# Second expert matrices on a DMA queue of their own, issued by GpSimd, in a two-block float32 kernel

## The reference, cut to what matters

```python
D_MODEL, N_EXPERTS, TOP_K, D_FF_2 = 1024, 32, 4, 1024
w1 = nrm((L, N_EXPERTS, D_MODEL, 2 * D_FF_2), D_MODEL ** -0.5)
w2 = nrm((L, N_EXPERTS, D_FF_2, D_MODEL), DEEPNORM_BETA * D_FF_2 ** -0.5)
...
f = moe_ffn(h.reshape(-1, D_MODEL), w_router[l], b_router[l], w1[l], b1[l], w2[l], b2[l]).reshape(x.shape)
x = layer_norm(DEEPNORM_ALPHA * x + gt2 * f, ln2_g[l], ln2_b[l])
```

## Time and profile before

| | |
|---|---|
| Time, median of 3 runs | 2309.51 us (2307.12 to 2314.98) |
| The profiled execution: its time, its span | 2312.77 us, 2311.0 us |
| TensorE busy over the span | 2213.1 us, 96% |
| VectorE, ScalarE, GpSimd busy | 706.0, 357.4, 100.3 us |
| Granted TensorE clock, mean | 0.979 |
| DMA, whole execution | 582.13 MB, mean 252 GB/s |
| DMA in the last 17 of 40 slices | 411 to 426 GB/s in all but the first and the last |

### The profile page before, as it was taken

The page is one execution under the profiler, slowest core; times in us unless marked ns, Lnnn a source line. Parts: engine busy times, 40 slices in busy tenths (PEclk is TensorE's granted clock), DMA queues, the critical chain, the costliest instruction groups (busy, mean ns, idle before and its releaser), DMA issues.

```text
span 2311.0 us, 34017 instructions
## 1 busy us (share of the span) xinstructions
PE 2213.1 (96%) x15007; PEld 1368.3 (59%) x15008; DVE 706.0 (31%) x1186; ACT 357.4 (15%) x771; POOL 100.3 (4%) x114
## 2 busy tenths in 40 slices
PE   7999999999999998989998998999999999999997
PEld 6767686888577775567887653344344444434432
DVE  0000101621275415347777532112111121121113
ACT  1000200240100012243434111001000010100000
POOL 1000000000100000112221000000000000000000
PEclk9999899999999999999999989999999999999999
DMA  9655444244678951000001379999999999999996
GB/s 319 192 158 184 145 138 145 82 137 161 221 237 273 285 189 55 1 3 3 3 22 48 149 313 419 426 426 424 417 424 426 425 426 411 417 425 426 425 425 271
DMA packets 199428, 582.13 MB, mean 252 GB/s; under 512 B 9620, under 2 KB 153808, under 8 KB 166384
## 3 DMA queue, kind: packets, MB, share of 16 engines
q1 hardware_dynamic: 194656, 564.70, 63.5%
q0 software_dynamic: 4208, 13.27, 1.5%
q10 hardware_dynamic: 416, 1.96, 0.2%
HBM read 576.49 MB, written 3.42 MB: 251 GB/s over the span
## 4 chain that ended last, share of the span: by engine, by line
PE 90%; DVE 5%; DMA 2%; ACT 1%; issue 1%; SPq 0%; ACTq 0%; DVEq 0%
PE ps L2561 22%; PE ps L605 13%; PE ps L2573 10%; PE ps L664 8%; PE ps L614 7%; PE ps L1333 5%; PE ps L2540 3%; PE ps L2588 2%; PE ps L795 2%; PE ps L768 2%; PE ps L1660 2%; PE ps L1680 1%; PE ps L1762 1%; PE ps L969 1%; DMA arena<-in_w 1%; PE ps L1677 1%
## 5 line engine op out<-in xcount | busy, mean ns | idle before, releaser
L2561 PE MATMUL ps<-ring,const 128*64 128x512 f32 (+1 forms) x1536 | 472.0, 594 | 0.8 <-ACT const L2315 0.8
L2561 PEld LDWEIGHTS ps<-ring,const 128*64 128x64 f32 (+1 forms) x1536 | 160.6, 144 | 307.4 <-issue 306.1
L605 PE MATMUL ps<-arena,ring 128*128 128x256 f32 x1408 | 313.4, 381 | 2.6 <-issue 2.6
L605 PEld LDWEIGHTS ps<-arena,ring 128*128 128x128 f32 x1408 | 264.7, 190 | 47.3 <-issue 12.9
L2561 PE MATMUL ps<-arena,const 128*64 128x512 f32 (+1 forms) x512 | 225.2, 593 | 0.0
L2573 PE MATMUL ps<-ring,const 128*64 128x512 f32 (+1 forms) x768 | 190.3, 594 | 0.8 <-DMA ring<-in_w 0.8
L664 PE MATMUL ps<-arena,ring 128*128 128x256 f32 x800 | 174.5, 381 | 1.3 <-issue 1.3
L664 PEld LDWEIGHTS ps<-arena,ring 128*128 128x128 f32 x800 | 153.0, 191 | 22.5 <-issue 1.5
L2775 DVE TENSOR_SCALAR arena<-ps 128x1024 f32<-128x1024 f32 x18 | 22.0, 1225 | 458.5 <-PE ps L2561 458.4
L614 PE MATMUL ps<-ring,arena 128*128 128x512 f32 x352 | 157.6, 592 | 0.0
L2573 PEld LDWEIGHTS ps<-ring,const 128*64 128x64 f32 (+1 forms) x768 | 65.2, 143 | 112.6 <-issue 111.1
(11 more groups left out here) (485 smaller groups left out, 2458.8 us busy)
## 6 DMA issues: line engine op xcount, KB each, us to landing
ring<-in_w SPq DMA_DIRECT2D x96, 2048.0 KB, 17.7
ring<-in_w SPq DMA_DIRECT2D x96, 1024.0 KB, 15.2
arena<-in_w SPq DMA_DIRECT2D x32, 2048.0 KB, 19.9
ring<-in_w_in SPq DMA_DIRECT2D x26, 1536.0 KB, 6.9
arena<-in_w SPq DMA_DIRECT2D x32, 1024.0 KB, 17.5
ring<-in_w_ada SPq DMA_DIRECT2D x16, 1536.0 KB, 9.0
ring<-in_ffn_w_gate SPq DMA_DIRECT2D x44, 512.0 KB, 4.0
ring<-in_ffn_w_up SPq DMA_DIRECT2D x44, 512.0 KB, 5.4
```

The lines of the kernel that those rows point to most:

```text
L605: ins = pe.matmul(ps[:, j % 2, half * S:(half + 1) * S], s[:, col0:col0 + P], uT[:, k, :], start=(k == 0), stop=(k == KD - 1))
L2561: ins = pe.matmul(ps[a * n:(a + 1) * n, q, :], xsT[:, k, a * n:(a + 1) * n], chunk(chunks[a])[:, q * 512:(q + 1) * 512], start=False, stop ...
```

## The change

The second matrices leave SyncE's list. A new function `moe_pool`, called last in GpSimd's program, goes through the blocks and issues their loads on GpSimd's own DMA queue (q0 in the profile; SyncE's is q1). Slots, chunk numbers, sizes and `room` stay as they are. The landings of second matrices are counted on eight semaphores of their own, one for each of the four chunk positions and for even and odd blocks; TensorE waits once for the chunks of both experts in place of once for each.

```diff
@@ chunk_tables
-        pieces += [W2_AT[s - 1] + i for i in range(KD // 2 * len(BLOCKS[s - 1]))] if s else []
@@ build
-        def w2_load(e, n, expert, c):
+        def w2_load(e, n, expert, c, landed_sem):
             e.dma_start(chunk(n).rearrange("p (j n) -> p j n", j=2),
-                        x["w2_2"][0, expert, 2 * c * P:2 * (c + 1) * P, :].rearrange("a (p j) n -> p (a j) n", j=2)).then_inc(*landing(n))
+                        x["w2_2"][0, expert, 2 * c * P:2 * (c + 1) * P, :].rearrange("a (p j) n -> p (a j) n", j=2)).then_inc(landed_sem, 16)
+
+        def second_landing(s, c):
+            return sems(f"w2_landed{s % 2}_{c}"), 16 * sum(len(BLOCKS[b]) for b in range(s % 2, s + 1, 2))
...
+        def moe_pool(e):
+            for s in range(NBLK):
+                blk = BLOCKS[s]
+                if s == 1:
+                    e.wait_ge(*at("cnt", 1))
+                expert = {}
+                for r in blk:
+                    expert[r] = bass.ds(e.value_load(ids[0:1, r:r + 1], min_val=0, max_val=NE - 1), 1) if s else slice(r, r + 1)
+                for c in range(KD // 2):
+                    for a, r in enumerate(blk):
+                        n = W2_AT[s] + c * len(blk) + a
+                        room(e, n)
+                        w2_load(e, n, expert[r], c, second_landing(s, c)[0])
@@ moe_sync
-                if s:
-                    blk = BLOCKS[s - 1]
-                    for c in range(KD // 2):
-                        for a, r in enumerate(blk):
-                            n = W2_AT[s - 1] + c * len(blk) + a
-                            room(n)
-                            w2_load(e, n, expert[r], c)
@@ moe_pe, second
-                    for a in range(w):
-                        moe_landed(pe, W2_AT[s] + c * w + a)
+                    pe.wait_ge(*second_landing(s, c))
@@ gpsimd
             load_last(p)
+            moe_pool(p)
```

More of the change, by code:

```diff
@@ L2479, in w1_load @@
                         x["w1_2"][0, expert, 2 * c * P:2 * (c + 1) * P, :].rearrange("a (p j) n -> p (a j) n", j=2)).then_inc(*landing(n))
-        def w2_load(e, n, expert, c):
+        def w2_load(e, n, expert, c, landed_sem):
             e.dma_start(chunk(n).rearrange("p (j n) -> p j n", j=2),
-                        x["w2_2"][0, expert, 2 * c * P:2 * (c + 1) * P, :].rearrange("a (p j) n -> p (a j) n", j=2)).then_inc(*landing(n))
-        def moe_sync(e, turns):
[L2486 to L2504, removed]
-                    if s:
-                        for r in blk:
-                            expert[r] = bass.ds(e.value_load(ids[0:1, r:r + 1], min_val=0, max_val=NE - 1), 1)
-                    for c in range(KD // 2):
-                        for a, r in enumerate(blk):
[L2510 to L2513, removed]
-                    blk = BLOCKS[s - 1]
-                    for c in range(KD // 2):
-                        for a, r in enumerate(blk):
-                            n = W2_AT[s - 1] + c * len(blk) + a
-                            room(n)
-                            w2_load(e, n, expert[r], c)
@@ new lines, in w2_load, with room @@
+                        x["w2_2"][0, expert, 2 * c * P:2 * (c + 1) * P, :].rearrange("a (p j) n -> p (a j) n", j=2)).then_inc(landed_sem, 16)
+        def second_landing(s, c):
+            return sems(f"w2_landed{s % 2}_{c}"), 16 * sum(len(BLOCKS[b]) for b in range(s % 2, s + 1, 2))
+        def room(e, n):
+            if n < 2:
+                pass
+            elif n < 8:
+                e.wait_ge(*at("v_end", 4))
+            elif n < 14:
+                e.wait_ge(*at("out2_0", 2))
+            elif n < MC:
+                e.wait_ge(*at("xhat", 2))
+            else:
+                e.wait_ge(*at("m_used", USED_AT[n - MC]))
@@ new lines, in moe_sync @@
+        def moe_sync(e, turns):
+            for s in range(NBLK):
+                blk = BLOCKS[s]
+                if s == 1:
+                    e.wait_ge(*at("cnt", 1))
+                expert = {}
+                for r in blk:
+                    expert[r] = bass.ds(e.value_load(ids[0:1, r:r + 1], min_val=0, max_val=NE - 1), 1) if s else slice(r, r + 1)
+                for c in range(KD // 2):
+                    for a, r in enumerate(blk):
+                        n = W1_AT[s] + 2 * (c * len(blk) + a)
+                        room(e, n + 1)
+                        w1_load(e, n, expert[r], c)
@@ L2526, in more @@
                 for c in range(KD // 2):
-                    w2_load(e, KD + c, one, c)
+                    w2_load(e, KD + c, one, c, sems(f"w_landed{2 * c + 1}"))
             moe_more(e, turns, most_tokens(e), more)
@@ L2698, in more @@
                 for c in range(KD // 2):
-                    more_landed(pe, KD + c, n)
+                    pe.wait_ge(sems(f"w_landed{2 * c + 1}"), n * 16 + (per_slot[2 * c + 1] + 16))
                     for ins in down_pe(pe, 1, c, KD + c):
```

## The result

The changed kernel takes 2350.92 us (median of 4 runs, 2344.51 to 2352.72) against 2308.44 us (median of 4) before: a ratio of 1.0176, 95% interval 1.0162 to 1.0190: 42.5 us more by the medians, 40.6 by the ratio. The profiled execution took 2351.81 us, with a span of 2350.1 us. So it is slower, by about the 41.3 us that were forecast. The lines of the changed kernel have moved: first-matrix loads are L2477, second-matrix loads L2481, the matmuls on them L2567 and L2579, the transposes of a block L2586.

A forecast was written before the change was run, and what follows sets the result against it. TensorE sets the pace, weights arriving just in time on full DMA engines. Delays 15.5 + 15.5 + 6, clock 7.5, less 3.2 give 41.3 us: 2309.5 + 41.3 = 2351 us, range 2314 to 2372, chance 0.62.

The forecast's parts named there:

- over 30 us: TensorE's DMA waits before second matmuls grow from 3.2 us to this, near 1705-1725, 2085-2105 and, smaller, 1505 us.
- 6 + 2.5: Block 1, before one-expert block 3: 6 us late, about the middle of 0 and 11.1, plus 2.5 us of clock.
- 15.5 + 2.5: Blocks 5 and 12, before one-expert blocks 7 and 14: 15.5 us late each, plus 2.5 us of clock each.
- 19.9 us of passing: Block 5: all 8.4 MB of block 7's first matrices pass at 422 GB/s, delaying the last second matrix this long.
- The clock term: After each of three new stalls the granted clock falls, losing 2.5 us: 7.5 us in all, 0 if it stays.
- The end: Last blocks: a later TensorE gives the transfers time, so the 3.2 us of waits there vanish.
- the places before two-expert blocks: Second matrices with a two-expert block following, as block 4: 11 us of delay against 13.7 of slack, taken as 0.
- the prediction's own rule: Before one-expert blocks: first matrices issued behind second ones pass them, two bytes for one, costing the delay beyond the slack.
- 0 for GpSimd's issuing: GpSimd: 128 issues of about 0.59 us and register loads, 76 us on an engine idle after 1398 us; cost 0.
- A: Whole stage: no difference, perhaps 3 us gained at the end as the 3.2 us of waits go; 2306 to 2310 us; 0.14.
- B: Milder: second queue gets more turns or half of block 7's loads pass, 5.6 us late twice; 2317 to 2323 us; 0.12.
- C: Worse: second matrices get a fifth, so five places before two-expert blocks add 20 us; 2370 us; chance 0.12.

The follow-up runs named there:

- block 5 put back: Changed kernel with only block 5's eight second-matrix loads given back to SyncE at their old place in its order; 2342.53 us, ratio 1.0151.
- the roles swapped: Kernel before, with first matrices from block 2 on issued by GpSimd and all second ones by SyncE; 2339.69 us, ratio 1.0142.
- tried alone: Kernel before with only the second matrices of the last two blocks (16 of 128 loads) on GpSimd's queue; 2314.26 us, ratio 1.0023.

## Why the prediction was right

*What bounds the kernel, and where the cost would be:* right. The total rate did not fall while both queues had work (424 GB/s), the issues fell when they did before (1691.29 us for block 5's last one, 1682.6 + 8.0 us of shift = 1690.6), and all but 0.3 us of the loss in the stage lies at blocks 1, 5 and 12. The sign "over 30 us" of waits in front of second matmuls was missed by a little: they are 29.0 us.

*The size of one step.* The sum's terms can be checked one by one, since the last load, its issue and the matmuls behind it are all in the chain. The first column is the landing after, less the landing of the earlier trace rows moved by what TensorE was late already (by the marks and the entry, -1.5, +8.0 and +24.7 us). The second is the same landing less the moment when TensorE wanted the load, moved in the same way; the third is what the 16 matmuls behind it took over 3.47 us, and the step is the sum of these two:

| | Passed, us | Late, us | Clock, us | Step, us | Predicted |
|---|---|---|---|---|---|
| Block 1 | 1511.1 - 1494.6 = 16.5 | 1511.1 - 1503.4 = 7.7 | 5.32 - 3.47 = 1.9 | 9.6 | 6 + 2.5 |
| Block 5 | 1732.0 - 1713.3 = 18.7 | 1732.0 - 1717.7 = 14.3 | 5.77 - 3.47 = 2.3 | 16.6 | 15.5 + 2.5 |
| Block 12 | 2107.0 - 2088.3 = 18.7 | 2107.0 - 2092.6 = 14.4 | 6.03 - 3.47 = 2.6 | 17.0 | 15.5 + 2.5 |

The forecast had 19.9 us of passing where a whole one-expert block's first matrices get through, and 18.7 was measured twice: nearly all of them pass. The clock term was 2.5 us and came out at 1.9 to 2.6. The granted clock of the changed kernel, in the 7 us from 1722 us on and from 1732 us on (columns as in the earlier trace rows):

```profile
1722.00:1729.00 7.00, 5.50 (x16) 1.32 (x12) 0.00 (x0) 0.00 (x0) 0.80 (x2) 0.70 1.00 425
...
1732.00:1739.00 7.00, 6.91 (x25) 2.73 (x26) 1.06 (x2) 0.00 (x0) 0.50 (x1) 0.69 1.01 419
```

It fell twice at block 5, once behind each of its two waits; the first fall lies inside the lateness of the last load and costs nothing more. The end gave back 2.5 us of the 3.2. The sum was 41.3 us; the steps and the end make 40.6 (43.1 - 2.5), the medians 42.5, the ratio 40.6. Block 1 came out 1.1 us above its term and blocks 5 and 12 1.0 to 1.4 us below theirs, so part of the closeness is errors that cancel. The remaining differences are smaller than the spread of the runs.

*What was right only by the kernel's luck.* The forecast took 0 for the places before two-expert blocks and for block 8. In the changed kernel that holds. For blocks 6, 8, 13 and 15 it holds because the stalls in front give the loads behind them time: with those at blocks 1, 5 and 12 taken away, steps of 9.6 us stand at blocks 6 and 13, and with these gone too, 5.5 us at block 8 and 4.6 us at block 15. My argument for 0 was another one, worked out at block 4 alone (11 us of delay against 13.7 of slack). It was not wrong there: no run with 8 KB second rows shows a step at block 4. But the other blocks I had not looked at.

Block 8 was left out by mistake. One-expert block 10 comes behind it, so by the prediction's own rule it is a fourth place like the three, and the prediction counted it among those before two-expert blocks. In the kernel before, these are the last two loads of block 8's second matrices, the first loads of block 10, and TensorE's second matmuls of block 8:

```profile
L2482 SPq DMA_DIRECT2D arena<-in_w x2: 332/332/333, 1835.6 to 1836.1; - x2
DMA to landing us min/median/max: 12.9/14.9/16.8
...
L2478 SPq DMA_DIRECT2D ring<-in_w x3: 332/332/333, 1841.9 to 1848.8; - x3
...
1852.78 13.88 PE ps L2573 x64
```

The last load lands at 1836.1 + 16.8 = 1852.9 us and is wanted at 1852.8 + 10.4 = 1863.2, a slack of 10.3 us. When block 10's loads start, 1852.9 - 1841.9 - 1.5 = 9.5 us of second matrices are left, at two for one 19.0 us of delay: 8.7 us late, 11.2 with the clock, and the sum would have been 52.5 us. In the changed kernel nothing of this was paid; 5.5 us came to light only when no stall stood before it. The omission and the time given by the stall cancel in the number.

Block 6 had little slack as well. Its last loads of second matrices and TensorE's second matmuls on them, before:

```profile
L2482 SPq DMA_DIRECT2D ring<-in_w x2: 332/1718/3103, 1713.3 to 1713.9; - x2
DMA to landing us min/median/max: 29.0/30.0/30.9
...
1750.49 13.88 PE ps L2573 x64
```

They land at 1713.9 + 30.9 = 1744.8 us and are wanted at 1760.9, a slack of 16.1 us, while block 8's first loads come from 1726.1 us on, with 17.2 us of second matrices still to come. Two for one could make that up to 34 us of delay; TensorE waited 7.4 us there once the stall at block 5 was gone. These later loads are issued one by one as slots come free, which may be why it was no more.

*The start of a load.* The forecast took 0 for GpSimd's issuing and allowed SyncE's loads 1.5 us to start. Both queues took about 3.5 us under load; block 7's first load in the changed kernel, issued at 1697.0 us, had its first packet 3.0 us later. With 3.0 us in place of 1.5 there are 13.8 us of second matrices left, at two for one 27.6, still more than block 7's 19.9 us, so it moved little. Block 1 was taken at the middle of 0 and 11.1 us for want of a better argument, and TensorE waited 7.7 us there in the changed kernel's profile, 4.5 with block 5 put back and 2.8 with the roles swapped.

*The rivals.* A (no difference) rests on the rule of the Trainium skill ("DMA: Bandwidth & Descriptors", "Issuing engines are not separate DMA queues") that loads issued from several engines interleave on the same DMA engines and save issue time only. The trace agrees on the rate, 424 GB/s with two queues. What the rule leaves open is the order, and here the order is 41 us. A's own place, the end, was tried alone and cost 5 to 7 us. B and C gave the second matrices another share than a third, or let only half of block 7's loads pass. The packets, 256 to 256, and the 18.7 us of delay where 19.9 is a whole one-expert block rule both out for this kernel, and with other rows a fifth and a half appear as the law of packets says.

## What to carry to other kernels

Where transfers and the engine that uses them are both near full, the order of the transfers is a schedule, and one queue keeps it. Here a second queue added no rate (424 GB/s against 422): it let late-wanted loads pass early-wanted ones, in the ratio of the packets' sizes. Before splitting, read for each load the time from landing to use and the bytes issued behind it that will share with it; and when a stall has been removed, read the slack of the loads behind it again, since the stall was giving it to them.

## What was not expected of the hardware

The exactness of the turns: 256 to 256, 254 to 254, 239 to 238, 223 to 224 and 290 to 288 packets between a queue fed by SyncE and one fed by GpSimd, for rows of 8 beside 16 KB, 4 beside 16 and 8 beside 8. And the start of a load: on idle engines SyncE's issue at 1369.41 us of the kernel before had its first packet at 1370.40 us, 1.0 us later; while the other queue kept the engines full it took 3.4 to 3.6 us for SyncE and 3.6 to 3.8 us for GpSimd.
